# A strided walk over the token columns in the w_in and w_out matmuls of a hybrid decoder layer

## What is computed

```python
h = rmsnorm(x, norm_mix_g)
proj = jnp.einsum('btd,de->bte', h, w_in)                 # 2048 x 3072
... # causal conv, RG-LRU scan, gelu gate, causal pooling, pool matmuls
y_mix = jnp.concatenate([y_lru, y_pool], axis=-1)
x = x + jnp.einsum('bte,ed->btd', y_mix, w_out)           # 2048 x 2048
h2 = rmsnorm(x, norm_mlp_g)
f = jax.nn.relu(jnp.einsum('btd,df->btf', h2, w_up))      # 2048 x 8192
x = x + jnp.einsum('btf,fd->btd', f * f, w_down)          # 8192 x 2048
y = rmsnorm(x, norm_final_g)
```

## Time and profile before

| what | us |
|---|---|
| median of three runs | 1843.9 |
| span of the profiled execution | 1841.4 |
| what lies around the span, by the median | 2.5 |
| TensorE matmuls in flight | 1812.1 (98%) |
| VectorE busy | 1478.1 (80%) |
| ScalarE busy | 924.6 (50%) |
| GpSimd busy | 132.9 (7%) |

### The profile page before, as it was taken

How to read it: one execution, slowest core, us unless ns; L and a number is a source line. 1 busy time by engine, 2 the same in 40 slices (tenths; PEclk the granted TensorE clock), 3 DMA queues, 4 the chain that set the end, 5 groups by cost and what they waited for, 6 DMA issues and landing times. The chain is left out here.

```text
span 1841.4 us, 38079 instructions
## 1 busy us (share of the span) xinstructions
PE 1812.1 (98%) x15016; PEld 1805.0 (98%) x15016; DVE 1478.1 (80%) x2039; ACT 924.6 (50%) x1322; POOL 132.9 (7%) x224
## 2 busy tenths in 40 slices
PE   7999999999999999999999999899999999999998
PEld 7999999999999999999999999899999999999998
DVE  7777785545488888888888888899888888889897
ACT  6555533333344454454445445555555555556565
POOL 3000000200000000000000000110000000001100
PEclk9999999999999999999999999999999999999999
DMA  8333333344354444544444452788666776767742
GB/s 275 103 92 91 97 98 93 116 152 139 99 171 148 160 146 163 173 135 156 148 161 146 143 173 90 213 233 238 185 179 179 199 181 181 192 168 206 230 114 93
DMA packets 209979, 288.19 MB, mean 157 GB/s; under 512 B 9437, under 2 KB 186089, under 8 KB 209808
## 3 DMA queue, kind: packets, MB, share of 16 engines
q1 hardware_dynamic: 185552, 186.75, 33.0%
q0 software_dynamic: 23984, 99.19, 18.7%
q10 hardware_dynamic: 288, 0.11, 0.0%
HBM read 222.00 MB, written 64.53 MB: 156 GB/s over the span
## 5 line engine op out<-in xcount | busy, mean ns | idle before, releaser
L897 PE MATMUL ps<-forms,u_high 128*128 128x260 f32 x2688 | 490.4, 282 | 0.7 <-DVE product_parts L1833 0.7
L897 PEld LDWEIGHTS ps<-forms,u_high 128*128 128x128 f32 x2688 | 413.0, 188 | 0.9 <-issue 0.9
L897 PE MATMUL ps<-forms,u_low 128*128 128x260 f32 x1344 | 374.8, 282 | 0.6 <-DVE u_low L1823 0.6
L897 PE MATMUL ps<-forms,d_high 128*128 128x260 f32 x2240 | 373.6, 283 | 1.0 <-DVE product_parts L1833 1.0
L897 PEld LDWEIGHTS ps<-forms,d_high 128*128 128x128 f32 x2240 | 314.4, 188 | 1.2 <-ACT d_high L1180 1.1
L897 PE MATMUL ps<-f_forms,d_high 128*128 128x260 f32 x1344 | 265.4, 283 | 4.2 <-ACT d_high L1180 1.6
L897 PEld LDWEIGHTS ps<-forms,u_low 128*128 128x128 f32 x1344 | 250.7, 188 | 0.8 <-DVE u_low L1823 0.8
L1363 DVE TENSOR_TENSOR w_low<-raw,w_high 128x512 fp32r<-128x512 f32 x160 | 109.0, 689 | 137.0 <-ACT w_high L992 135.8
L897 PEld LDWEIGHTS ps<-f_forms,d_high 128*128 128x128 f32 x1344 | 204.9, 188 | 6.7 <-ACT d_high L1180 3.7
L897 PE MATMUL ps<-forms,d_low 128*128 128x260 f32 x1120 | 192.5, 283 | 0.0
L992 ACT ACTIVATE w_high<-raw 128x512 fp32r<-128x512 f32 x160 | 99.4, 628 | 180.7 <-PE ps L704 174.6
(11 more groups left out here) (305 smaller groups left out, 3578.5 us busy)
## 6 DMA issues: line engine op xcount, KB each, us to landing
even_rows<-in_w_up_dram SPq DMA_DIRECT2D x32, 1024.0 KB, 5.6
odd_rows<-in_w_up_dram SPq DMA_DIRECT2D x32, 1024.0 KB, 5.8
d_even<-in_w_down_dram SPq DMA_DIRECT2D x33, 768.0 KB, 7.1
d_odd<-in_w_down_dram SPq DMA_DIRECT2D x33, 768.0 KB, 5.2
raw<-in_w_in_dram SPq DMA_DIRECT2D x96, 256.0 KB, 2.7
sums_spill<-part_out POOLq DMA_DIRECT2D x40, 520.0 KB, 5.4
scratch<-f_spill POOLq DMA_DIRECT2D x20, 910.0 KB, 7.1
f_spill<-f_out POOLq DMA_DIRECT2D x32, 520.0 KB, 4.7
```

What stands on the lines that cost most here:

```text
L897: mm = pe.matmul(out, w[:, k, :], x[:, form, :], start=(PRODUCT_OPENS[r] and at == 0), stop=at == len(steps) - 1, skip_group_check=True)
```

## The change

Every moving operand and every output of the three matmuls of `unit` gets another order of columns. The 260 columns are 65 groups of four neighbours (16 bytes). `by_lines` views them as 13 x 5 x 4 and walks them as 5 x 13 x 4: in a sweep every fifth group of four, thirteen of them, and five such sweeps. Input and output are walked alike, so that each column's result lands where it did. The fillers become 42: seven each of six patterns, the first with 272 columns, the others with 260, read from the first set from element 260 on: steps of four, thirteen and five groups in sweeps, the last two of these also with the sweeps' order reversed, and one walk over every fourth group of 260. Their output is written in a row into `BANK_D`.

```diff
+LINE_STEP = 5
-WARM = 14 * (512,) + 24 * (128,)
...
         def _(pe):
+            def by_lines(half):
+
+                return half.rearrange("p (m n e) -> p n m e", n=LINE_STEP, e=4)
+
             def unit(n, j, buf, high, low):
...
                         for a in range(2):
-                            out = ps[:, 4 * buf + 2 * t + a, 0:HALF]
-                            pe.matmul(out, wh, high[:, k, a * HALF:(a + 1) * HALF], start=first, stop=False)
+                            out = by_lines(ps[:, 4 * buf + 2 * t + a, 0:HALF])
+                            pe.matmul(out, wh, by_lines(high[:, k, a * HALF:(a + 1) * HALF]), start=first, stop=False)
                         for a in range(2):
-                            out = ps[:, 4 * buf + 2 * t + a, 0:HALF]
-                            pe.matmul(out, wh, low[:, k, a * HALF:(a + 1) * HALF], start=False, stop=False)
+                            out = by_lines(ps[:, 4 * buf + 2 * t + a, 0:HALF])
+                            pe.matmul(out, wh, by_lines(low[:, k, a * HALF:(a + 1) * HALF]), start=False, stop=False)
                         for a in range(2):
-                            out = ps[:, 4 * buf + 2 * t + a, 0:HALF]
-                            mm = pe.matmul(out, wl, high[:, k, a * HALF:(a + 1) * HALF], start=False, stop=last)
+                            out = by_lines(ps[:, 4 * buf + 2 * t + a, 0:HALF])
+                            mm = pe.matmul(out, wl, by_lines(high[:, k, a * HALF:(a + 1) * HALF]), start=False, stop=last)
...
-            for n in WARM:
-                x = s_high[0][:, S3:S3 + (2 if n > HALF else 1), 0:min(n, PROMPT // 2)]
-                pe.matmul(ps[:, BANK_D, 0:n], s_high[0][:, A11, 0:P], x, start=True, stop=True)
+            first_set = s_high[0].rearrange("p r t -> p (r t)")
+            for times, w, x in (
+                (7, first_set[:, 0:P], first_set[:, 260:532].rearrange("p (l s e) -> p s l e", s=4, e=4)),
+                (7, first_set[:, 0:P], first_set[:, 260:520].rearrange("p (l s e) -> p s l e", s=13, e=4)),
+                (7, first_set[:, 0:P], first_set[:, 260:520].rearrange("p (l s e) -> p s l e", s=5, e=4)),
+                (7, first_set[:, 0:P], first_set[:, 260:520].rearrange("p (l s e) -> p s l e", s=13, e=4)[:, ::-1]),
+                (7, first_set[:, 0:P], first_set[:, 260:520].rearrange("p (l s e) -> p s l e", s=5, e=4)[:, ::-1]),
+                (7, first_set[:, 0:P], first_set[:, 260:1300].rearrange("p (l s e) -> p l s e", s=4, e=4)[:, :, 0, :]),
+            ):
...
+                for _ in range(times):
+                    pe.matmul(into, w, x, start=True, stop=True)
```

More of the change, by code:

```diff
@@ L902, in _ @@
             pe.wait_ge(s_hi, 2)
-            for n in WARM:
-                x = s_high[0][:, S3:S3 + (2 if n > HALF else 1), 0:min(n, PROMPT // 2)]
-                pe.matmul(ps[:, BANK_D, 0:n], s_high[0][:, A11, 0:P], x, start=True, stop=True)
+            first_set = s_high[0].rearrange("p r t -> p (r t)")
[7 more added lines that the diff above has]
+            ):
+                into = ps[:, BANK_D, 0:x.shape[1] * (x.shape[2] if len(x.shape) > 2 else 1) * (x.shape[3] if len(x.shape) > 3 else 1)]
+                if len(x.shape) == 3:
+                    into = into.rearrange("p (a b) -> p a b", b=x.shape[-1])
+                if len(x.shape) == 4:
+                    into = into.rearrange("p (a b c) -> p a b c", b=x.shape[-2], c=x.shape[-1])
+                for _ in range(times):
+                    pe.matmul(into, w, x, start=True, stop=True)
             for m in range(UP_PAIRS):
```

## The result

The changed kernel takes 1904.31 us, the median of three runs (1903.02 to 1905.85): 1.0334 times the kernel before, with a 95% interval of 1.0316 to 1.0353. It is slower by about 60 us, where no change was forecast (1843.0) and the range ended at 1895.

A forecast was written before the change was run, and what follows sets the result against it. TensorE's matmul spacing was taken to bound w_in and w_out. Matmuls 0 plus fillers 0 meant no change from the profiled 1841.4 us span and 1843.9 us median: forecast 1843.0 us, with an 8-in-10 range of 1815 to 1895.

The forecast's parts named there:

- What bounds the kernel: In w_in and w_out, from about 40 to 510 us, time is the number of matmuls times their 119.0 ns spacing.
- The count of exposed matmuls: Of w_in's and w_out's 3840 matmuls, 3648 counted for a gain, as the first pair partly waits for loads.
- the matmuls' patterns: Term for the 3840 walked matmuls of w_in and w_out: taken as 0, with about 2 us either way.
- The row chosen as nearest: The same 260 columns at various addresses, 116.7 to 120.8 ns a matmul, mean 119 in w_in and w_out.
- bounds of -33 and +437 us: Limits for the 3840 matmuls: 9 ns less on 3648, or each jumped-to group taking twice its slot, 114 ns a matmul.
- The slower rival: Each group-to-group step costs, in the columns' read or accumulating write: +113 us, 1956, at one slot each; chance 0.31.
- If only the four turns cost: Slower rival's variant, only turns to a sweep's start cost: +7 us (1851) at one slot each, +71 (1915) at ten.
- The faster rival: Jumps part the columns' and weights' reads where they meet: 1835.5, 1827.5 or 1811 us, put at 1829; chance 0.33.
- The two rules on PSUM: Skill rules: any non-contiguous pattern slows matmuls significantly, or neighbouring pairs suffice and groups of four cost nothing.
- The fillers: Between w_out and the first product: 42 fillers take 5.0 us instead of 5.87, hidden by the u_low wait; term 0.
- The chances: No change 0.36, faster 0.33, slower 0.31, with 0.19 beyond 1895 us for jumps costing half a slot or more.

The follow-up runs named there:

- reading alone: The changed kernel with the strided walk on the moving operand only, PSUM written in a row: 1906.4 us, ratio 1.0349 to the kernel before.
- writing alone: The changed kernel with the strided walk on the PSUM output only, moving operand read in a row: 1842.1 us, ratio 1.0000 to the kernel before.
- fillers alone: Only the change's fillers, w_in's and w_out's matmuls as in the kernel before: 1842.2 us, ratio 1.0003.
- thirteen backwards: Kernel before, w_in's and w_out's reads and writes in thirteen sweeps of five groups, all backwards: 1839.9 us; with w_up and w_down too: 1822.95 us.

## Why the prediction was wrong

- **What bounds the kernel** was right: TensorE's spacing in w_in and w_out goes to the end one for one, less the first pair. The count of exposed matmuls is 3648: reading alone lost 64.7 us, and 64.7 / 0.0179 = 3610. The prediction used it for gains and 3840 for losses.
- **The step that failed** is the value for the matmuls' patterns: "A permutation of whole groups meets as many groups as before, on average at as many bad moments. I take 0". It measured +17.9 ns a matmul, 65 us. The row chosen as nearest, the same 260 columns at various addresses, varied the start of the walk and never its step. In the trace before, the chunks of a pair run through 116.8, 119.0, 119.6, 120.2, 119.4, 119.5, 119.1 and 118.6 ns and then through the same eight again. A chunk is 130 groups, so the start modulo 16 groups repeats every eight chunks, but so does the weights' slot, and which of them makes this pattern is not shown. The averages that agreed within 0.9 ns were all averages of one step, 1. They said nothing about another, and between bounds of -33 and +437 us such a row should not have narrowed the range.
- **The slower rival** had the right place, the read's step from group to group, as one of its two, and its price at a whole slot a step (29 ns, 1956 us) was 1.6 times what was measured (17.9 ns, 1904 us). Its form was wrong: the same cost is not paid for every jump. By it the 5-step walk and the 4-step walk had to cost alike; they cost 18 and 2 ns. "If only the four turns cost" fell too: turns are steps like others, here 5 modulo 16.
- **The faster rival**, streams that meet, fell as the cause: with a quarter of the weights the dear walks cost the same. That an order exists which is better than the row was right, though at 0.5 ns instead of 2.3 or more in these stages.
- **The two rules on PSUM.** The strict one of the Trainium skill, "PSUM — Partial Sum Buffer", Specifications, doesn't hold here: writing alone cost nothing (ratio 1.0000). The looser sentence of the Trainium skill, "Advanced Engine Details and Errata", Memory Cachelines, agrees with this measurement; the prediction took it for all that this section asks, but the strict sentence stands in it too. The rule of the same section of the Trainium skill for SBUF, two hits on a line of 16 bytes, does not hold: walks with four hits a line cost from 118.6 to 166 ns by their step, and pairs, two hits a line, cost double.
- **The fillers** were right: nothing was lost by them (fillers alone: ratio 1.0003). They ran 5.5 us where 5.0 was forecast, covered by the wait for u_low.
- **The chances** gave slower 0.31, and 0.19 to more than 1895. The range's upper end was drawn where jumps cost 0.2 ns each; no row of before stood for that limit, and the measured time lies 9 us beyond it.

## What to carry to other kernels

When fp32 matmuls read 260 columns in another order, look at the step between groups of 16 bytes modulo 256 bytes: here 1, 2, 3, 4, 7, 9, 11, 12, 14, 15 cost 118.5 to 122 ns, 8 and 10 cost 128, and 5, 13, 0 and 6 cost 137 to 166. Where a walk mixes steps, measure it: their costs did not add up. The output was walked likewise for nothing in the two orders tried, five sweeps and thirteen backwards. Keep at least four fp32 neighbours together and start on 16 bytes. An average over addresses is no evidence for another access pattern; a cheap way to get that evidence is to give each repeated stage of one kernel a pattern of its own, with the unchanged stages beside it as the measure.

## What the runs showed of the hardware

- The moving operand's read costs by its step with a period of 16 groups (256 bytes), the same for single walks up to 26 groups apart and for sweeps that keep one step modulo 16, and not the same in both directions (+6: 166 ns, -6: 127.8).
- Costs of mixed steps do not add up: thirteen sweeps in reversed order cost 126.7 ns, where 136.0 would follow from the single steps.
- A row is not the best order: step 3 saves 0.5 ns of 119.0 in w_in and w_out, 2.0 of 119.9 in w_up and 1.5 of 119.9 in w_down, 1.1% of this kernel.
- Writing PSUM in five sweeps of groups of four costs nothing: 119.0 ns, ratio 1.0000.
- A weight load with each fp32 element in a 16-byte group of its own holds the spacing at 235 to 239 ns, at a granted clock of 0.50 and of 1.00 alike; with two in a group the row is at 121.2 instead of 119.0.
- Single columns and pairs double the spacing, to 232.5 and 233.1 ns.
